# One-hot rows of the expert picks: both halves in one comparison on VectorE, the gate factor multiplied in on ScalarE

## What is computed

```
s1, s2 = scores of a token against two sets of 128 keys, per head (8 heads)
v1, i1 = top_k(s1, 16);  v2, i2 = top_k(s2, 16)
top_s, pos = top_k(v1[:, None] + v2[None, :], 16)
idx  = (i1 * 128 + i2) at pos;   gate = softmax(top_s)
act  = gelu(x . expert_u[idx])
y    = sum over heads and picks of gate * act * expert_v[idx]
x    = layer_norm(alpha * x + y)
```

## Time and profile before

| | |
|---|---|
| median of three runs | 2994.18 us |
| the profiled execution: own time, span | 2987.0 us, 2984.8 us |
| busy: TensorE, VectorE, ScalarE, GpSimd | 88%, 78%, 41%, 33% of the span |
| moved by DMA | 1100.78 MB, mean 369 GB/s |
| the 22 steps with one-hot groups | 2267 to 2467 us, 200 us |
| busy in them: TensorE, VectorE, ScalarE | 185.9, 187.4, 82.1 us |

### The profile page before, as it was taken

How to read it: one execution, slowest core, us unless ns; L and a number is a source line. 1 busy time by engine, 2 the same in 40 slices (tenths; PEclk the granted TensorE clock), 3 DMA queues, 4 the chain that set the end, 5 groups by cost and what they waited for, 6 DMA issues and landing times. The chain is left out here.

```text
span 2984.8 us, 53582 instructions
## 1 busy us (share of the span) xinstructions
PE 2625.5 (88%) x20678; PEld 1536.0 (51%) x20678; DVE 2327.1 (78%) x4875; ACT 1221.7 (41%) x3050; POOL 991.8 (33%) x888
## 2 busy tenths in 40 slices
PE   9999988787887767768888879999999987999997
PEld 7777433232332333323333336666677775767774
DVE  7965577999879899976767877777777993777777
ACT  3354143333345555533433433333334432544554
POOL 0000144444446555544343532332232322111112
PEclk9999999889996777779998999999999998999999
DMA  4113699999999999999999999999999999999996
GB/s 167 64 57 141 241 407 420 415 418 418 408 420 417 417 415 420 418 420 421 419 420 409 420 420 396 391 408 402 404 418 364 414 424 358 369 370 387 383 402 272
DMA packets 175384, 1100.78 MB, mean 369 GB/s; under 512 B 17830, under 2 KB 34342, under 8 KB 52779
## 3 DMA queue, kind: packets, MB, share of 16 engines
q0 software_dynamic: 110592, 805.36, 65.7%
q1 hardware_dynamic: 64554, 292.16, 24.8%
HBM read 1061.79 MB, written 35.65 MB: 368 GB/s over the span
## 5 line engine op out<-in xcount | busy, mean ns | idle before, releaser
L994 POOL DMA_INDIRECT arena_high<-uv_dram,idx_now x768 | 953.0, 1241 | 1629.8 <-PE ps L1285 1488.4
L2461 DVE SCALAR_TENSOR_TENSOR arena_high<-arena_low,arena_high 128x1024 f32<-128x1024 f32 x768 | 922.6, 1223 | 260.8 <-DMA arena_high<-uv_dram,idx_now 254.9
L1285 PE MATMUL ps<-arena_high 32*32 32x512 f32 x12288 | 489.7, 667 | 259.4 <-ACT arena_high L1846 256.8
L1523 PE MATMUL ps<-arena_low 128*128 128x256 f32 x2048 | 464.9, 383 | 14.5 <-DMA arena_low<-ut_dram 14.5
L1523 PEld LDWEIGHTS ps<-arena_low 128*128 128x128 f32 x2048 | 385.5, 191 | 123.9 <-issue 61.3
L1837 ACT ACTIVATE gcol<-hcol 128x2 f32<-128x2 f32 x384 | 77.5, 202 | 855.3 <-DVE arena_high L2461 854.7
L1285 PEld LDWEIGHTS ps<-arena_high 32*32 32x32 f32 x12288 | 93.8, 107 | 456.9 <-ACT arena_high L1846 363.6
L1246 PE MATMUL ps<-arena_low 128*128 128x512 f32 (+1 forms) x512 | 241.3, 614 | 0.0
L347 PE MATMUL ps<-wv_hi_bytes,w_hi_bytes 128*128 128x512 f32 x512 | 207.8, 406 | 18.5 <-DVE x_hi_bytes L2585 7.2
L1846 ACT ACTIVATE arena_high<-arena_high,wcol 128x32 f32<-128x32 f32 x768 | 204.8, 314 | 12.6
L349 PE MATMUL ps<-wv_hi_bytes,w_lo_bytes 128*128 128x512 f32 x512 | 203.3, 397 | 0.0
(11 more groups left out here) (266 smaller groups left out, 4035.4 us busy)
## 6 DMA issues: line engine op xcount, KB each, us to landing
arena_low<-ut_dram SPq DMA_DIRECT2D x64, 1024.0 KB, 10.0
arena_high<-vt_dram SPq DMA_DIRECT2D x32, 1024.0 KB, 10.2
arena_low<-vt_dram SPq DMA_DIRECT2D x32, 1024.0 KB, 10.4
arena_low<-spread_dram SPq DMA_DIRECT2D x32, 512.0 KB, 9.1
acts_dram<-arena_low SPq DMA_DIRECT2D x14, 1024.0 KB, 13.7
arena_low<-acts_dram SPq DMA_DIRECT2D x28, 512.0 KB, 7.2
arena_low<-slabs_dram SPq DMA_DIRECT2D x11, 1152.0 KB, 9.8
arena_high<-uv_dram,idx_now POOLq DMA_INDIRECT x768, 12.4
```

Source lines behind the costliest of these rows:

```text
L994: pool.indirect_dma_start(out=ring[:, s % RING, :], out_offset=None, in_=uv_d, in_offset=bass.IndirectOffsetOnAxis(ap=idx_now[:, s:s + 1], ...
L1285: last = nc.tensor.matmul(ps[out:out + QUAD, y_bank(t // PH) + turn, :], diag[rows, s % DIAGS, :], ring[rows, s % RING, cs], start=fresh, ...
L1523: last = nc.tensor.matmul(ps[:, 5 + n % 4 // 2, o:o + 2 * P], u_slot[n % USLOTS][:, k, :], x1T[:, BLK - DENSE:BLK, k, :], start=(k == 0), ...
L2461: last = nc.vector.scalar_tensor_tensor(out=ring[:, s % RING, 0:D], in0=x1[c][:, j, :], scalar=1.0, in1=ring[:, s % RING, 0:D], op0=ALU.mu ...
```

## The change

One VectorE instruction compares all 1024 columns of a group (rows and columns of the picks, four tokens) with `iota128`. ScalarE then multiplies the row half by the gates in place, four instructions of 128 columns per group, and only after that TensorE may use the group. ScalarE does this behind the copies of the same step, for the groups of the next step. The halves of `hot` change places; the products are the same.

```
--- before.py
+++ after.py
@@ -613,6 +613,7 @@
         picks_turned = Again(v_done, 4)
         picks_ready = Again(v_read, 4)
         hot_ready = Again(att_kq_done, 32)
+        hot_weighted = Again(z_late, 32)
         g_psum = Again(av_done, 16)
         g_read = Again(out_read, 4)
         g_stored = [Again(wv_in, 16), Again(bv_in, 16)]
@@ -1527,14 +1528,14 @@
 
             def g_group(i):
 
-                wait_again(pe, hot_ready, i + 1)
+                wait_again(pe, hot_weighted, i + 1)
                 if i == 0:
                     wait_again(pe, picks_ready, DENSE)
                 if i >= 2:
                     wait_again(pe, g_read, i - 1)
                 for q in range(4):
-                    last = nc.tensor.matmul(ps[:, (4, 7)[i % 2], q * P:(q + 1) * P], hot[i % HOTS][:, q, 0:P],
-                                            hot[i % HOTS][:, q, P:2 * P], start=True, stop=True, skip_group_check=True)
+                    last = nc.tensor.matmul(ps[:, (4, 7)[i % 2], q * P:(q + 1) * P], hot[i % HOTS][:, q, P:2 * P],
+                                            hot[i % HOTS][:, q, 0:P], start=True, stop=True, skip_group_check=True)
                 last.then_inc(g_psum.sem, 1)
 
             def v_tile(n):
@@ -1988,6 +1989,16 @@
                 nc.scalar.activation(act_out[c % 2][:, i:i + 2, :].rearrange("p a b -> p (a b)"), ps[:, 5 + n % 4 // 2, :],
                                      ACT.Gelu).then_inc(act_ready.sem, 1)
 
+            def hot_weight(i):
+
+                wait_again(act, hot_ready, i + 1)
+                j = i // (P // 4)
+                t0 = 4 * i - j * P
+                for q in range(4):
+                    last = nc.scalar.activation(hot[i % HOTS][:, q, 0:P], hot[i % HOTS][:, q, 0:P], ACT.Copy,
+                                                scale=picksT[:, j, 2, t0 + q:t0 + q + 1])
+                last.then_inc(hot_weighted.sem, 1)
+
             def g_group(i):
 
                 wait_again(act, g_psum, i + 1)
@@ -2039,6 +2050,10 @@
                 if 0 <= o < G_STEPS:
                     for i in range(g_first(o), g_first(o + 1)):
                         g_group(i)
+                o = s - G_STEP0 + 1
+                if 0 <= o < G_STEPS:
+                    for i in range(g_first(o), g_first(o + 1)):
+                        hot_weight(i)
                 v = s - U_STEPS
                 if -1 <= v < V_STEPS:
                     for n in range(v_first(v) + AHEAD if v >= 0 else 0, min(v_first(v + 1) + AHEAD, NT)):
@@ -2553,13 +2568,10 @@
                     wait_again(dve, g_psum, i - HOTS + 1)
                 j = i // (P // 4)
                 t0 = 4 * i - j * P
-                nc.vector.tensor_tensor(hot[i % HOTS][:, :, 0:P], iota128[:, :].unsqueeze(1).to_broadcast([P, 4, P]),
-                                        picksT[:, j, 1, t0:t0 + 4].unsqueeze(2).to_broadcast([P, 4, P]), ALU.is_equal)
-                for q in range(4):
-                    t = t0 + q
-                    last = nc.vector.tensor_scalar(hot[i % HOTS][:, q, P:2 * P], iota128[:, :], picksT[:, j, 0, t:t + 1],
-                                                   picksT[:, j, 2, t:t + 1], ALU.is_equal, ALU.mult)
-                last.then_inc(hot_ready.sem, 1)
+                nc.vector.tensor_tensor(hot[i % HOTS].rearrange("p q (h e) -> p q h e", e=P),
+                                        iota128[:, :].unsqueeze(1).unsqueeze(1).to_broadcast([P, 4, 2, P]),
+                                        picksT[:, j, 0:2, t0:t0 + 4].rearrange("p h q -> p q h").unsqueeze(3).to_broadcast([P, 4, 2, P]),
+                                        ALU.is_equal).then_inc(hot_ready.sem, 1)
 
             def dense(G):
 
```

## The result

| | before | after |
|---|---|---|
| median | 2995.61 us (6 runs, 2992.81 to 3002.02) | 3003.89 us (6 runs, 3002.07 to 3007.42) |
| ratio after / before | | 1.0029 [1.0018, 1.0040] |
| profiled execution: own time, span | 2987.0, 2984.8 us | 3002.43, 3000.3 us |

The change makes the kernel slower by 0.29%, some 8 us. The profiled execution of before was a low one, 8.6 us under its median, so the two spans differ by more than the runs do. That is why the stage is compared by its own steps here, and each kernel was traced a second time (e9, e10).

A forecast was written before the change was run, and what follows sets the result against it. VectorE and TensorE were near their limit beside a full DMA, VectorE costing the path only some 5 us. Terms -4.7 + 0 + 4.3 + 4.9 - 2.5 = +2.0 us on 2994.2 gave 2996 us, range 2984 to 3012.

The forecast's parts named there:

- the ScalarE rival: Slower, ScalarE becomes the bound between a step's last copy and the next expert weights: 3005.5 us; chance 0.32.
- VectorE: One-hot rows: one comparison replaces five instructions, 0.49 us saved a group; dot products come earlier, -4.7 us on the path.
- A multiplication's price: ScalarE's four new multiplications a group: 0.30 us each, 1.2 us a group, 3.6 us a step, 77 us in the stage.
- The ring in common steps: Third group, copy, multiplications, expert weights, next first copy: 7.33 us, covered by TensorE's 7.58 us step, so 0.
- Table reloads: ScalarE's table loads for Sqrt and Exp lengthen the ring past TensorE's step: +4.3 us together.
- steps 4 and 5: Step from 2297.73: Sqrt and Exp make 12.8 us of ring, against 11.1 before, +1.7 us.
- The second Exp's step: ScalarE's second Exp with its two table loads: 7.3 + 2.9 against TensorE's 7.58, +2.6 us.
- Store waits: When ScalarE stands for a store, the next step's multiplications stand behind it and delay TensorE: +4.9 us together.
- Its own formula: After a landing: copy 0.6, multiplications 3.6, weights 1.28, copy 0.6, so 6.1 us until the third group of 1.13.
- Given back: Delay between a store's issue and landing only shortens ScalarE's wait, and stores land earlier on the full DMA: -2.5 us.
- The third Exp: ScalarE's third Exp with table loads lies ahead of the 10.18 us store wait, which covers it: 0.

The follow-up runs named there:

- e9: The kernel before, unchanged, traced a second time: 193.40 us for the 22 steps that make one-hot groups, in an execution of 2990.7 us.
- e10: The changed kernel, unchanged, traced a second time: 205.55 us for the 22 steps that make one-hot groups, in an execution of 3003.77 us.
- e4: Against the kernel before: ScalarE multiplies as in the change, VectorE keeps its five instructions, without the gate; 3005.2 us, ratio 1.0031.
- e6: The change with eight multiplications of 64 columns a group in place of four of 128: 3028.57 us, ratio 1.0117 to the kernel before.
- e3: The change without ScalarE's multiplications and their wait, gate factor left out: 2992.31 us, ratio 0.9987 to the kernel before.
- e7: The kernel before with only half of each block's columns stored and read back twice: 2984.76 us, ratio 0.9971 to the kernel before.
- e8: The change with only half of each block's columns stored and read back twice: 2992.83 us, ratio 0.9997 to the kernel before.

## Where the forecast held and where it failed, step by step

The range of 2984 to 3012 us holds the result, but by luck: it reaches 3003.9 only through the weight given to the ScalarE rival, whose mechanism the runs do not show.

**VectorE: right.** It is relieved as forecast (1.14 to 1.17 us a group for 1.14), and the path gains 4.2 us for 4.7. The reason given, that at this size an instruction's fixed cost outweighs its columns, holds in part: without the gate the four small ones still take 0.78 us (e4), where 512 columns more in the new comparison take 0.53 to 0.56; the other 0.24 us was the gate as an operand, which no row of before showed apart.

**A multiplication's price: right.** Twelve take 3.50 us to the next instruction, 1.17 us a group for 1.2. The Trainium skill, ScalarE: Activation LUTs, section What ACT_TABLE_LOAD costs, gives 186 ns, 93 for a pointer operand and 0.833 a column, less 93 of overlap: an estimate of 386 ns alone and 293 in a row. The trace agrees, with 392 and 292; the Trainium skill would have given this price where no row of before showed it.

**The ring in common steps: right, at 0.** They stay at 7.52 to 7.74 us. e6 shows that the ring is real. The rival "ScalarE becomes the bound" gave 3005.5, nearest to the time, but by a mechanism that is not there: it needs 1.28 us a group, and 1.17 was measured; its sign is steps of 8 us or more throughout, and the common ones are not.

**Table reloads: right in the sum, by luck in its parts.** The sum is +4.1 for +4.3 in the steps of the Sqrt and the first two Exps, with half stores as well (+3.8). But steps 4 and 5, around the Sqrt, lose 3.2 us for 1.7: step 4 takes 13.3 us for the 12.8 forecast, and 10.4 before in the mean of two traces, not 11.1. The second Exp's step loses 0.9 for 2.6. The forecast set a ring of three groups against a step of 7.58 us; this step has two groups, 6.51 us before, and eight multiplications, as the chain of the changed kernel shows:

```profile
2377.98 2.32 ACT arena_low L1998 x8
```

**Store waits: right in mechanism at two landings, mis-sized.** 4.9 was forecast, 10.8 came. These two landings make most of the difference.

At the landing of 2429.8 the forecast took 1.6 us, the mean of the two others. Its own formula, 6.1 us from the landing to the third group and 1.13 for it, gives the end at 2437.05 in the change, where the trace has 2436.85. In the kernel before, the third group there ended 4.5 us after the landing of 2423.54, since weighted rows of three groups lay ready; that step lost nothing in spite of a wait of 3.37:

```profile
2425.10 2.96 PE L1536 MATMUL ps<-arena_low 128*128 128x128 f32 x24
```

So 7.23 - 4.5 = 2.7 was to be had from the trace of before, in place of a mean. The rest is a landing 0.6 us later in the step and half-clock work behind it (the experts in 1.94 us for 1.14).

At the last landing the third group starts after 7.0 us and not 6.1 (2462.54 to 2469.57): two copies stood ahead of the multiplications and a Gelu behind the weights, which the formula left out, 0.9 us. Then the third group took 2.05 us for 1.13 and the experts 2.01 for 1.14, at half the clock, 1.8 us. With the 1.0 forecast that is the 3.7 by which the way from the landing to the next step grew (10.95 us for 7.26). The forecast priced waits and no clock, though the earlier trace rows held the sign: 24 products in 5.46 us behind the wait of 4.98, and eight in 2.05.

The rest of the 10.8 is at the first landing, +3.0 for +2.3. Near as it is, it does not bear the mechanism out: e3 loses 3.2 there without multiplications, its landing 6.2 us into step 7, for 5.3 and 2.5 in the two traces of before, and 4.88 us for 16 products of a tile behind it where 3.72 is usual. What the multiplications add there is open.

**Given back: wrong, 0 in place of -2.5.** The step that failed is the claim that the delay falls between a store's issue and its landing, and so only shortens ScalarE's wait. Most of the delay lies ahead of the issue. SyncE's timeline of the kernel before:

```profile
2417.72 15.43 SPq L863 DMA_DIRECT2D arena_low<-ut_dram  x2
2433.19 0.91 SPq L872 DMA_DIRECT2D spread_dram<-arena_low  x2
```

And of the change:

```profile
2423.39 20.19 SPq L864 DMA_DIRECT2D arena_low<-ut_dram  x2
2443.62 0.91 SPq L873 DMA_DIRECT2D spread_dram<-arena_low  x2
```

The store stands behind a load of `u` tiles that waits for TensorE to finish with a slot. In the change the block is complete at 2425.84 and its store is issued at 2443.62, right as the `u_tile` of the next step but one ends. What a step loses, that issue loses. Measured from the first step's start it came 7.0 us later than before (its last part at 2444.10 less 2276.15, against 2433.67 less 2272.73), landed 18.4 us after its issue for 19.3 before, and so was 6.1 us late. In the chain's other two stores, too, issue to landing is as before: 17.4 and 17.1 us, for a median of 17.5. A full DMA that is asked for less (385 GB/s for 402 in the second traces) landed the last one 0.9 us sooner behind its issue, and the others no sooner.

The third Exp, on the other hand, was covered, as forecast. It comes after that issue (2450.16), so it cannot move the landing: from the start of step 19 to the landing it is 23.9 us in the change and 24.0 before, and ScalarE's wait shrank from 10.18 to 7.70 us. This wait covered what came between the issue and the landing, and not what came ahead of the issue.

**The sum.** Of 9.2 us missed (11.2 - 2.0), 5.9 are the store waits, 2.5 the part given back, 0.5 each the VectorE term and the other steps; the reloads were 0.2 over.

**What stays open.** Whether the store's place in the queue or its size makes it late was not separated: issuing each block's store ahead of the load of `u` tiles was not run. The timed distance of e7 and e8 is unexplained, and with it the timed runs do not rule out that ScalarE's work costs wherever it stands; only the traces speak against it.

## What to carry to other kernels

- An engine that is 40% busy has room, but not at every place. Work put behind a wait that ends late lengthens everything that is released after it: price it at the table reloads and the landings, not by the sum of busy time. The same 256 multiplications, with VectorE's relief, made the traced stage 11 us longer behind all of a step's copies and 2 us longer between them (0.29% and 0.17% in the timed runs, whose intervals overlap).
- An engine on the chain that ended last need not be worth its time there: VectorE held 44 us of it, and relieving it won 2 to 4 us, since in e3 TensorE and a gather hold the same stretch.
- Before a wait is counted as a cover, look at what sets its end. If the transfer is issued by a queue that follows the delayed engine, a delay ahead of the issue moves both ends and is not covered; one between issue and landing is.
- A wait on TensorE costs twice where the granted clock falls with it, as at the last landing here: add the products that run at half speed behind it.

## What the runs showed of the hardware that was not expected

- A second per-partition operand costs VectorE time: 345 ns with key and gate, 284 with the key and a constant (e4), for 128 columns.
- An activation of 64 columns in a row of its kind takes 0.24 us, one of 128 0.29 (e6): halving the columns saves less than a fifth.
- Behind one wait of 4.12 us TensorE's granted clock was 0.50 for 8.5 us, and half of the whole stage's loss (5.4 of 11.2 us) is products that took longer, not waits.
